# Two ring slots in place of three, and ten weight pieces kept in place of nine

## The reference, cut to what matters

```python
h = _rmsnorm(x, norm1_g[l])
proj = h @ w_in[l]
...
x = x + mixed @ w_out[l]
h2 = _rmsnorm(x, norm2_g[l])
x = x + _peer(h2, peer_w_q[l], peer_sub_keys[l], peer_u[l], peer_v[l])
...
u = expert_u[it]
vv = expert_v[it]
act = jax.nn.gelu(jnp.einsum('thkd,td->thk', u, xt), approximate=False)
return jnp.einsum('thk,thkd->td', gt * act, vv)
```

## Time and profile before

| | us |
|---|---|
| median of 3 runs | 2883.33 |
| lowest and highest | 2882.97, 2887.86 |
| span of the profiled execution | 2882.3 |
| busy: TensorE, VectorE, GpSimd, ScalarE | 2249.1, 1985.7, 1211.1, 1094.7 |

### The profile page before, as it was taken

How to read it: one execution, slowest core, us unless ns; L and a number is a source line. 1 busy time by engine, 2 the same in 40 slices (tenths; PEclk the granted TensorE clock), 3 DMA queues, 4 the chain that set the end, 5 groups by cost and what they waited for, 6 DMA issues and landing times. The chain is left out here.

```text
span 2882.3 us, 29016 instructions
## 1 busy us (share of the span) xinstructions
PE 2249.1 (78%) x9210; PEld 1025.9 (36%) x9210; DVE 1985.7 (69%) x4782; ACT 1094.7 (38%) x3164; POOL 1211.1 (42%) x1037
## 2 busy tenths in 40 slices
PE   9888989778977887778976898878898655655555
PEld 6535525343542343333542244333354111111111
DVE  3857766787666578787667666888666666666654
ACT  2333423552333345562333334666233322222222
POOL 0332434444443334454443343555344444445443
PEclk9999999989998998889998899899999787677777
DMA  9999999999999999999999999999999999999998
GB/s 387 359 418 404 413 419 419 416 406 411 407 421 420 419 419 409 421 420 411 420 421 420 412 407 417 391 422 421 415 420 421 421 419 416 419 415 419 416 420 356
DMA packets 180009, 1188.02 MB, mean 412 GB/s; under 512 B 19984, under 2 KB 21648, under 8 KB 48784
## 3 DMA queue, kind: packets, MB, share of 16 engines
q0 software_dynamic: 147456, 1073.81, 90.2%
q1 hardware_dynamic: 32400, 112.36, 9.9%
HBM read 1181.90 MB, written 4.19 MB: 412 GB/s over the span
## 5 line engine op out<-in xcount | busy, mean ns | idle before, releaser
L632 POOL DMA_INDIRECT ring<-table_uv,idx_t x1024 | 1209.2, 1181 | 1651.3 <-PE acc L900 1390.1
L1461 DVE CUSTOM_DVE_ANT_0 ring<-ring,h2r 128x1024 f32<-128x1024 f32 x1024 | 1249.3, 1224 | 783.7 <-DMA ring<-table_uv,idx_t 779.6
L900 PE MATMUL acc<-ring,wmask 128*64 128x512 f32 x4096 | 1211.9, 720 | 570.5 <-ACT wmask L1058 569.4
L900 PEld LDWEIGHTS acc<-ring,wmask 128*64 128x64 f32 x4096 | 283.6, 154 | 1285.1 <-ACT wmask L1058 850.0
L1053 ACT ACTIVATE dots<-dots 128x2 f32<-128x2 f32 x512 | 104.1, 203 | 1531.9 <-DVE dots L1461 1530.9
L1058 ACT ACTIVATE wmask<-gmask,dots 128x64 f32<-128x64 f32 x1024 | 300.3, 340 | 48.6 <-ACT dots L1053 1.5
L1046 ACT ACTIVATE gmask<-stack,gate_t 128x64 f32<-128x64 f32 x1024 | 293.1, 334 | 0.1
L655 PE MATMUL pt<-hT,w_ring 128*128 128x256 f32 (+1 forms) x480 | 99.4, 360 | 3.3 <-issue 3.1
L1053 ACT ACT_TABLE_LOAD x73 | 93.7, 1283 | 1.3
L655 PE MATMUL pt<-hT,w_held 128*128 128x256 f32 (+1 forms) x480 | 93.7, 344 | 0.0
L646 PE MATMUL pz<-w_ring,hT 128*128 128x512 f32 x192 | 91.6, 620 | 0.0
(11 more groups left out here) (272 smaller groups left out, 2173.4 us busy)
## 6 DMA issues: line engine op xcount, KB each, us to landing
w_ring<-wstream SPq DMA_DIRECT2D x131, 512.0 KB, 8.0
ring<-wstream SPq DMA_DIRECT2D x32, 512.0 KB, 13.2
ring<-table_uv,idx_t POOLq DMA_INDIRECT x1024, 12.5
w_held<-wstream SPq DMA_DIRECT2D x9, 512.0 KB, 15.0
xs<-x_in_dram SPq DMA_DIRECT2D x8, 512.0 KB, 7.7
h2r<-wstream SPq DMA_DIRECT2D x8, 512.0 KB, 14.1
scores<-wstream SPq DMA_DIRECT2D x8, 512.0 KB, 15.0
xs<-wstream SPq DMA_DIRECT2D x4, 512.0 KB, 11.9
```

The costliest lines, as they stand in the source:

```text
L632: nc.gpsimd.indirect_dma_start(out=ring[:, t % SLOTS, :], out_offset=None, in_=table, in_offset=bass.IndirectOffsetOnAxis(ap=idx_t[:, q, i ...
L900: mm = nc.tensor.matmul(acc[HALF * i:HALF * i + HALF, half * 512:(half + 1) * 512], wmask[:, slot, :], ring[:, slot, D + half * 512:D + (h ...
L1461: d = V.tensor_tensor_reduce(u, u, h2r[:, b % H_SLOTS, i, :], 1.0, 0.0, ALU.mult, ALU.add, dots[:, t % SLOTS:t % SLOTS + 1])
```

## The change

Two constants change. The ring has two slots, and the 512 KB that this frees hold one more piece for the whole run. Everything that is derived from them moves too:

```diff
-W_SLOTS = 3
+W_SLOTS = 2
...
-HELD = 9
+HELD = 10
...
 SPARE = 5
 TURN_OVER = SPARE + W_SLOTS
 X_AT = (28, 30)
 SPARE_END = 4 * TURN_OVER - W_SLOTS
 FIRST_HELD = PIECES - HELD
 FIRST_ROOM = FIRST_HELD - 6
```

## The result

The changed kernel takes 2903.59 us in the median of four runs (2899.64 to 2906.02), the kernel before beside it 2883.30 (2882.97 to 2887.86). The ratio is 1.006, with a 95% interval of 1.0048 to 1.0073: slower by 0.5 to 0.7%, about 17 us. (The ratio is not the quotient of the two medians, which lie 20.3 us apart.

The account below looks back on a forecast made before the run. Bound by DMA bytes from the first gather on. First gather +3.7, moved loads -2.7, end of stage 1 +4.2, two later loads -2.5, stages 2 to 4 0: +2.7, so 2886.0 us; range 2879.6 to 2894.5.

Parts of the forecast that it names:

- Stages 2 to 4: TensorE's short waits for ring loads in dense stretches are covered by the gathers: 0 us, at worst 3.
- about 5.5: TensorE's lag in us, added up over the first ten pieces of a stage in stages 2 to 4.
- 6.5 us of cover: In stage 4's tightest dense stretch gathers take 12.4 us against 5.9 at least, which should hide TensorE's lag.
- The third rival: Dense stretches of stages 2 to 4 stall the expert stream, up to 3 us each: +11.7, 2895; chance 0.06.
- End of stage 1: Pieces 28 to 31 land late through two slots; the lag less 3.8 us covered gives +4.2 us (0 to 10.2).
- L: TensorE's lag at the end of stage 1, put at 3 to 14 us and taken as 8.
- the case that the prediction named last: The prediction fails if a stage's serial part, not bytes, sets its pace; then each us of ring wait counts in full.
- Stage 0: Chain to the first gather: late pieces 34 to 37 delay the first gather by 3.7 us (2.6 to 4.5).
- Moved loads: Stage 1's pieces 29 to 31 no longer share the DMA engines between 239 and 254 us: -2.7 us (0 to 3.8).
- Bytes: One load fewer in each of stages 1 to 4, 126 loads and 2.1 MB less: 5.0 us at most.
- The sum: All terms together over the whole run: +2.7 us, giving a time of 2886.0 us.
- the upper end: Worst-case total of the terms over the whole run: +13 us, 2896.5.

Follow-up runs that it names:

- e7: The kernel before, with loads in stages 2 to 4 alone waiting for the stream piece two back instead of three: 2898.66 us, 1.0043.
- e11: The kernel before, with the two-deep wait only for the first twelve pieces of stages 2 to 4: 2896.52 us, 1.0040.
- e12: The changed kernel once more, unchanged, for a second measurement and profile: 2907.57 us, 1.0085 to the kernel before.
- e1: The kernel before with two ring slots instead of three, nine pieces still held: 2905.82 us, 1.0080.
- e3: The changed kernel with stage 0's pieces 32 to 37 put into the still empty gather ring: 2899.11 us, 1.0059 to the kernel before.
- e4: The changed kernel with stage 1's pieces 28 to 31 in spare places, loaded ahead: 2898.77 us, 1.0052 to the kernel before.
- e8: The kernel before with the two-deep wait in stage 0 alone: 2886.09 us, 1.0005.
- e2: The kernel before, with piece 32 not loaded in stages 1 to 4 and a held piece's weights used instead: 2880.93 us, 0.9988.
- e5: The kernel before once more, unchanged, for a second profile: 2883.47 us, 0.9996.
- e10: The kernel before with stage 0's pieces 32 to 37 put into the gather ring: 2886.05 us, 1.0003.

## Why the prediction was wrong, point by point

- **The step that failed: "Stages 2 to 4 ... I take 0, at worst 3."** It is 12.4 us (e7), most of it in the first twelve pieces (e11). What was wrong is the lag that it reckoned with, "about 5.5" over the first ten pieces of a stage. It took two mixes between release and need (7.4 us) for the usual case and one (5.5) for the exception. But a half step is 4 matmuls, and in the dense stretches mostly 12 of them lie between two mixes, as the earlier trace rows show. So between the end of piece m - 2 and the start of piece m mostly stand one mix and one piece, 5.6 us, against 8.0 to land and 9.4 in the case shown: 2.4 to 3.8 us short where 0.5 was the rule. TensorE's mixes fall behind by 12.2 us in the stretch of stage 2 (11.5 in e12, 11.2 in e7, 14.7 in e11), of it 9.8 in waits and 1.7 in slower matmuls, where 5.5 stood. The other half of the step, 6.5 us of cover, was about right: from dot 96 to dot 112 the dots lose 5.3 us (4.3, 5.6, 8.5), which is 5.6 to 7.2 less than the lag. In stages 3 and 4 of e7 the lag grows by 8.6 and 9.2 us, and the dots lose 2 to 4. The cover has no sharp edge, since the GB/s are down to 400 before the lag has passed 5.8 us. That the lag would be worked off was right too, but by then the transfers had been lost.
- **The third rival** named the place and the sign ("GB/s below 410 there would mean the third rival"), with 2895 against 2903.59 and a chance of 0.06. It let a lag of 5.5 us go uncovered; what happened was a lag of twice that, about half covered. The reason for the small chance, the cover, holds.
- **End of stage 1: the lag was right, its cover was not there.** L was taken as 8; the mixes fall behind by 9.3 us (8.0 in e12, 8.5 in e1, 7.5 in e3). Of it 3.8 were to be covered by gathers in flight, which left +4.2; but the dots lose all of it, 9.6. They can't win it back, since the mixes stay 13.2 us late for the next 40 us, on an engine that has next to no idle time there (in the kernel before it is busy for 39.8 of the 40.0 us from 290 to 330). This is the case that the prediction named last: where the serial part sets the pace, each us counts in full. The step had no term for slower matmuls, which are 3.7 of the 9.3. e4 takes 8.5 us out of the place. Over the whole run less of it counts: e4 and e3 together give 7 us or, against e12, 14.
- **Stage 0**: the first gather +3.7, measured +4.0, with the waits at pieces 34 to 37 as named, but for piece 36, and one more of 1.1 at piece 32. How much of it reaches the end is open: e3 gives nothing against the first measurement of the changed kernel and 7 us against e12, and e8 can't tell. "Nothing hides this" was too strong. In the six profiles whose stage 1 is that of the kernel before, but for one load in e2 (e2, e5, e7, e8, e10, e11), the first dot is 3.9 to 6.9 us late, mostly by ScalarE's stop, and 1.4 to 3.8 us of that are made up by dot 60.
- **Moved loads**: -2.7. Between the first dot and dot 48 the changed kernel makes up 4.5 us in one profile and 4.3 in e12, e1 4.2 and e3 3.1. The eight profiles without the moved loads (e2, e4 to e8, e10, e11) make up 0.5 to 1.7 there all the same. The rest is 1.4 to 4.0 us, so the term was right.
- **Bytes**: 2.1 MB and 126 loads as said, and 3.5 us of gain (e2) for at most 5.0.
- **The sum.** With e7's 12.4 for 0 and 9.6 for 4.2, the sum of 2.7 us becomes 20.5, between the two measured losses. That it fits so well is in part luck. After dot 96 the changed kernel's dots fall back by only 2.9 us more (6.1 in e12, 5.9 in e1), those of e7 by 11.3: the losses don't simply add up, and why they don't is open. Two smaller slips: the upper end took 1 us for stages 2 to 4, where the step itself says "at worst 3", and about 1.8 us, not 1.0, lie around the span in every execution for which both are on record.
- **The Trainium skill** ("Trainium Kernel Development and Optimization", Best Practices) asks for double-buffering so that DMA overlaps compute. With two slots the loads still overlap, and no run here supports that two are enough: at 8.0 us to land and 5.6 between release and need, e1 loses 23 us.

## What to carry to other kernels

For a ring of n slots, read the issue-to-landing time and the work that really stands between the release of a slot and its next use in the densest stretch, group by group in the timeline, mixes and half steps as they lie; if landing takes longer, the ring is too short, whatever the mean says. Here the usual case was taken for the exception, and the lag came out at half its size. Price the waits by place: 76 us of them in the dense stretches cost about as much as 182 over the run. The gathers in flight hid 5 to 7 us of TensorE's lag in stages 2 to 4 and none at the end of stage 1, where TensorE had no idle time to win it back. A wait of the engine that feeds the bottleneck can have a second price, where the matmuls after it run at the lower clock.

## What the runs showed of the hardware that was not expected

- **A wait can halve TensorE's clock for the work after it.** Four matmuls took 3.55 us after a wait of 3.95 us and eight took 5.66 after 3.58 (the first four of them at half speed), where eight take 3.70 at full clock. After a wait of 2.81 us the next twelve took 5.42, as in the earlier trace rows, so not every wait does it. The Trainium skill ("TensorE: Matmul & The Clock Gate", Part 1) says that the clock gate falls from 2.4 to 1.2 GHz when the array has been idle and rises when it has been busy; the rows agree, 0.89 us a matmul against 0.46. The mean granted clock of the whole run doesn't show it: 0.898 in the changed kernel, 0.883 before and 0.894 in e5. It counts where TensorE is already late.
- **ScalarE stops for 2.2 to 6.7 us**, one to three times between the first gather and the first dot, released by something that the profile doesn't show. It does so in 13 of 14 profiles, the unchanged kernel's (e5) among them, and not in the first profile of before. The cause is open.
- **DMA throughput sags step by step when the gathers are late**: 419, 400, 379, 321 GB/s in successive 10 us, while TensorE falls back by 5.8 and then 8.8 us and GpSimd waits up to 10.0 us for a mix. It then stands at 362 and 371, though the lag still grows to 12.2.
